# RMS norms moved in front of the feature-major projections, the last norm by token tile, and a first weight chunk that takes its tokens in halves

## The chip, the cores and the metric

The kernel runs on one core of a Trainium2 chip. The metric is the device time of one execution in microseconds (us). The kernel is one program with five engines that run side by side: TensorE (PE, with its weight loads as PEld), VectorE (DVE), ScalarE (ACT), GpSimd (POOL) and SyncE (SP), which issues most of the loads. They are kept in order by semaphores alone.

## The reference, cut to what matters

512 tokens of 1024 features pass through a first block (two attention layers with a mixture of experts, not touched here) and a second block of two layers. The second block, in float32, is

```python
for layer in range(DEPTH):                       # DEPTH = 2
    hn = rms_norm_2(h, norm_mix[layer])
    h = h + mixer(hn)                            # layer 0: retention and delta net; layer 1: rglru_mixer
    h = h + conv_ffn(rms_norm_2(h, norm_ffn[layer]), ffn_w_up[layer], ..., ffn_w_down[layer])
return rms_norm_2(h, norm_final)

def _rms(x):
    return x * lax.rsqrt(jnp.mean(x * x, axis=-1, keepdims=True) + EPS)
def rms_norm_2(x, gain):
    return _rms(x) * gain
```

`ffn_w_up` is 1024 x 5632, `ffn_w_down` 2816 x 1024 (22 rows of 128), `lru_w_in` 1024 x 2048.

## The kernel before, in words

The state X lies with tokens on the partitions: four tiles (T = 4) of 128 tokens x 1024 features. Every product of float32 matrices is made of three one-pass matmuls: each operand is split into a rounded part (hi) and a rest (lo), and `product` issues hi·hi, hi·lo and lo·hi. `raw(c)` and `hi(c)` are the two buffers of a weight chunk c: ACT rounds the raw chunk in two pieces (`round_chunk`), DVE puts the rest back over the raw one in two pieces (`rest_of_chunk`). There are two such pairs of buffers, so a chunk's load waits until the chunk before the last one is used up; SP issues it.

A feature-major projection (`linear_T`) keeps the weights still (128 x 128) and streams the 512 tokens, so it needs the normed X turned: XT (hi) and XH (lo) hold it as 8 blocks of 128 features by 512 tokens. Four places of the second block matter here, and I name them by letters:

- **A**: from `mix_out` (the last product of layer 0's mixer) to `ffn0_up`.
- **B**: from `ffn0_down` to `lru_in`, the first projection of layer 1's mixer.
- **C**: from `lru_out` to `ffn1_up`.
- **D**: from `ffn1_down` over the final norm to the store of `out`.

At A, B and C the order before is: DVE adds the last product to X (`residual`, `ffn_residual`), ACT squares all four tiles with a sum along the row (`squares`), POOL makes the reciprocal roots (`power`, L905 and L907), DVE multiplies each tile with its root into XH (`rms`, L2751), PE waits for all four tiles, bridged by some matmuls on constants (`keep_warm`, L1970), and turns them with 32 transposes (`turn`, L1795), one bank for each block of features over all tokens; ACT rounds each bank with the gain as its per-partition scale (`rounded_T`, L1111), DVE takes the rest (`rest_of_T`, L2678), and `linear_T` starts. The weights' first chunk is rounded on ACT before the squares and split on DVE before the scaling. A chunk of an up projection or of `lru_in` is four outputs of 24 matmuls with 512 columns.

`ffn` on PE then runs 11 chunks of up and, before the change, six chunks of down with 4, 4, 4, 4, 4 and 2 rows of 128; each chunk goes over four token tiles and two halves of the 1024 features, and `down_used` tells SP that a chunk is used up. The down product's left operand is `act` (rest) with `act_hi(f)`: rows 0 to 6 have their hi in a buffer `hi`, rows 7 to 14 in XT, rows 15 to 21 in XH.

At D the final norm scales by root and gain in one instruction (L3701) for each tile after all four are added, and one DMA stores all of `out`.

The PSUM banks are given out by a planner (`plan.take`, `plan.pick`), in turn.

## Time and profile before

| | |
|---|---|
| median of 3 runs | 3312.08 us (3310.1 to 3312.66) |
| span of the profiled execution | 3301.4 us |
| between the span and the median | 10.7 us, ahead of the first and after the last instruction |
| PE busy | 3133.6 us, 95% of the span |
| DVE, ACT, POOL busy | 2171.0, 1594.0, 415.7 us |
| mean granted TensorE clock | 0.982 |

The profiled execution has a span but no time of its own beside the three runs, so its own time is taken to be its span and the 10.7 us around it. "Start" in the rows is counted from the start of the span. L numbers are lines of the kernel before unless a row is said to be of the changed one, whose lines lie 10 to 70 further down.

### The profile page before, as it was taken

Reading aid. Unit: us, or ns where it says so; the run is one execution under the profiler, and the core shown is the slowest. Engines: PE = TensorE matmul, PEld = TensorE weight load, DVE = VectorE, ACT = ScalarE, POOL = GpSimd, SP = SyncE. Lnnn points to the kernel's source line nnn. Section 1 sums busy time; section 2 is a strip of 40 time slices with the busy share of each in tenths; the row PEclk is TensorE's granted clock in tenths of the full one; section 3 lists DMA queues with packets and bytes.
Section 4 is the critical chain, followed back from the end, with each engine's and each line's share of the span. In section 5 each row is a group of like instructions: output and inputs, shape, how many; then the busy total and the mean of one; then the engine's idle time right before and its main releaser. Section 6 shows DMA issues by size and latency. Waiting matters only on the chain.

```text
span 3301.4 us, 39275 instructions
## 1 busy us (share of the span) xinstructions
PE 3133.6 (95%) x14815; PEld 2391.1 (72%) x14815; DVE 2171.0 (66%) x2380; ACT 1594.0 (48%) x1889; POOL 415.7 (13%) x274
## 2 busy tenths in 40 slices
PE   8879999999998989899999999998899999999998
PEld 7556667777776867577777757877788887788886
DVE  2375578888885266688888876564477745757653
ACT  2465167777774344477777754342322212722211
POOL 0000122222212000222223220010000000000000
PEclk9999999999999999999999999999999999999999
DMA  7200389999993211699999973330123223223321
GB/s 263 106 1 14 149 309 361 351 358 360 359 355 134 77 46 65 249 363 348 356 361 351 360 279 73 76 65 1 60 94 98 82 101 102 77 83 102 102 102 64
DMA packets 174479, 599.20 MB, mean 181 GB/s; under 512 B 25571, under 2 KB 74899, under 8 KB 124947
## 3 DMA queue, kind: packets, MB, share of 16 engines
q1 hardware_dynamic: 140528, 541.75, 44.9%
q0 software_dynamic: 23472, 51.42, 4.4%
q10 hardware_dynamic: 10355, 4.33, 0.5%
q8 instruction: 83, 1.36, 0.2%
q14 instruction: 41, 0.34, 0.0%
HBM read 581.17 MB, written 48.23 MB: 191 GB/s over the span
## 4 chain that ended last, share of the span: by engine, by line
PE 78%; DVE 8%; DMA 6%; ACT 4%; issue 3%; POOL 1%; DVEq 0%; SPq 0%; ACTq 0%; POOLq 0%
PE bank L1820 20%; PE bank L1822 19%; PE bank L1821 19%; DMA ring<-w_gate 3%; PE bank L1832 3%; PE bank L2368 2%; PE bank L1884 2%; PE bank L1885 2%; PE bank L2118 1%; PE bank L1827 1%; PE bank L1828 1%; DVE st L2779 1%; PE bank L1945 1%; ACT ring_rounded L1276 1%; PE bank L2149 1%
## 5 line engine op out<-in xcount | busy, mean ns | idle before, releaser
L1821 PE MATMUL bank<-ring_rounded,big_rounded 128*96 128x512 f32 (+1 forms) x1680 | 660.1, 393 | 0.0
L3019 DVE TENSOR_TENSOR ring_rounded<-ring,big_rounded 128x2048 fp32r<-128x2048 f32 x252 | 568.1, 2287 | 42.2 <-ACT big_rounded L1276 41.3
L2666 DVE TENSOR_TENSOR ring_rounded<-ring,ring_rounded 128x2048 fp32r<-128x2048 f32 (+2 forms) x124 | 273.4, 2247 | 402.0 <-ACT ring_rounded L1096 401.9
L1276 ACT ACTIVATE big_rounded<-ring 128x2048 fp32r<-128x2048 f32 x252 | 478.6, 1918 | 74.2 <-DMA ring<-w_up 56.6
L1096 ACT ACTIVATE ring_rounded<-ring 128x2048 fp32r<-128x2048 f32 (+2 forms) x124 | 226.7, 1878 | 454.9 <-DMA ring<-ffn_w_down 163.6
L1820 PE MATMUL bank<-big_rounded 128*96 128x512 f32 x992 | 395.0, 398 | 1.0 <-DVE ring_rounded L3019 0.8
L3019 DVE TENSOR_TENSOR ring_rounded<-ring,ring_rounded 128x2048 fp32r<-128x2048 f32 x128 | 292.6, 2287 | 156.4 <-ACT ring_rounded L1276 148.1
L1822 PE MATMUL bank<-big_rounded,XH_rounded 128*96 128x512 f32 x992 | 392.1, 395 | 0.0
L1821 PEld LDWEIGHTS bank<-ring_rounded,big_rounded 128*96 128x96 f32 (+1 forms) x1680 | 277.5, 165 | 105.4
L1276 ACT ACTIVATE ring_rounded<-ring 128x2048 fp32r<-128x2048 f32 x128 | 245.1, 1916 | 208.3 <-DMA ring<-w_gate 208.0
L1822 PE MATMUL bank<-ring_rounded,XH_rounded 128*96 128x512 f32 (+1 forms) x776 | 307.2, 396 | 0.0
L1820 PE MATMUL bank<-ring_rounded,big_rounded 128*96 128x512 f32 (+1 forms) x688 | 276.2, 401 | 11.8 <-DVE XH_rounded L3028 4.9
L1820 PE MATMUL bank<-XT_rounded,ring_rounded 128*128 128x512 f32 x696 | 274.1, 394 | 2.4 <-DVE big L3108 2.4
L1821 PE MATMUL bank<-XH_rounded,ring_rounded 128*128 128x512 f32 x696 | 271.6, 390 | 0.0
L1822 PE MATMUL bank<-XT_rounded,ring_rounded 128*128 128x512 f32 x696 | 271.4, 390 | 0.0
L1820 PE MATMUL bank<-ring_rounded,XT_rounded 128*128 128x512 f32 (+1 forms) x584 | 228.7, 392 | 9.4 <-DVE XH_rounded L3450 3.9
L1822 PE MATMUL bank<-ring_rounded,big_rounded 128*128 128x512 f32 (+1 forms) x608 | 235.7, 388 | 0.0
L956 POOL DMA_INDIRECT expert_rows<-big,idx x64 | 118.2, 1847 | 865.8 <-ACT big L1298 809.3
L1821 PE MATMUL bank<-ring_rounded,XT_rounded 128*128 128x512 f32 (+1 forms) x584 | 227.0, 389 | 0.0
L1822 PEld LDWEIGHTS bank<-big_rounded,XH_rounded 128*96 128x96 f32 x992 | 159.8, 161 | 70.3
L1820 PEld LDWEIGHTS bank<-big_rounded 128*96 128x96 f32 x992 | 162.2, 164 | 66.9 <-DVE ring_rounded L3019 1.7
L905 POOL TENSOR_SCALAR st<-st 128x1 f32<-128x1 f32 (+3 forms) x43 | 16.4, 382 | 1523.0 <-ACT lnp L1355 918.6
(464 smaller groups left out, 5238.1 us busy)
## 6 DMA issues: line engine op xcount, KB each, us to landing
ring<-w_up SPq DMA_DIRECT2D x128, 1024.0 KB, 7.6
ring<-w_down SPq DMA_DIRECT2D x128, 1024.0 KB, 7.8
ring<-w_gate SPq DMA_DIRECT2D x128, 1024.0 KB, 7.0
ring<-ffn_w_up SPq DMA_DIRECT2D x44, 1024.0 KB, 6.9
ring<-ffn_w_down SPq DMA_DIRECT2D x10, 2048.0 KB, 7.8
ring<-ret_gdn_w_in SPq DMA_DIRECT2D x8, 2048.0 KB, 13.3
expert_rows<-lnp POOLq DMA_DIRECT2D x1, 12288.0 KB, 40.2
ring<-odd_w_qkv SPq DMA_DIRECT2D x6, 2048.0 KB, 8.0
```

Of the source, the lines that this page charges most:

```text
L956: pool.indirect_dma_start(expert_rows, bass.IndirectOffsetOnAxis(ap=used[0:CAP, e:e + 1], axis=0), M["YE"][0:CAP, e % 2, :], None, bounds_ ...
L1096: act.activation(one_pass(hi(c)[:, ks, :]), raw(c)[:, ks, :], ACT.Copy).then_inc(rounded[c.pair], 1)
L1276: act.activation(one_pass(expert_hi(j)), expert_raw(j), ACT.Copy).then_inc(signal("half_rounded").sem, 1)
L1820: pe.matmul(dst, x_hi, y_hi, start=first, stop=False)
L1821: pe.matmul(dst, x_hi, y_lo, start=False, stop=False)
L1822: return pe.matmul(dst, x_lo, y_hi, start=False, stop=last)
L1832: return pe.matmul(dst, one_pass(x_hi), one_pass(y_lo), start=False, stop=last)
L1884: pe.matmul(dst, w, one_pass(XT[:, kk, :].rearrange("p (t c) -> p t c", t=T)), start=(kk == 0), stop=False)
L1885: pe.matmul(dst, w, x_lo, start=False, stop=False)
L2368: ins = pe.matmul(ps(u)[:, tokens(h)], lhsT[:, h, :], rhs[:, h, :], start=start and (stop or h == 0), stop=stop and (start or h == GDN_HEA ...
L2666: dve.tensor_tensor(one_pass(w), w, parts(hi(c)[:, ks, :]), ALU.subtract).then_inc(split[c.pair], 1)
L3019: dve.tensor_tensor(one_pass(expert_raw(j)), expert_raw(j), parts(expert_hi(j)), ALU.subtract).then_inc(signal("half_split").sem, 1)
```

## The change

At A, B and C the norm is made tile by tile, with root and gain in one DVE instruction (`scaled_by_row`); the gain row comes by a POOL DMA into `lnp[:, 0, :]` (`load_gain`). Each tile is turned by 8 transposes into two banks of its own (`turn_tile`), and PE issues those of tiles 0, 1 and 2 behind tiles 1, 2 and 3 of the product that ends the stage before. The first chunk of the next projection (`first_T_by_halves`) runs its first three outputs over tokens 0 to 255 with 256-column matmuls, turns tile 3 behind the second of them, runs the same three over tokens 256 to 511, and the fourth over all 512. The constants' matmuls are gone. At D adding and scaling alternate by tile and each tile is stored by a DMA of its own. The down rows go in chunks of 3, 3, 4, 4, 4, 4; the last four rows keep their hi in `hi`, so XH is free for the next norm, and DVE waits for two used chunks before it writes them.

```diff
+DOWN_ROWS = [(0, 3), (3, 3)] + [(f, 4) for f in range(6, KF, 4)]
...
-        U["rmsf0_T"] = plan.take(KD)
+        U["rmsf0_T"] = [plan.pick(b) for b in (0, 1, 2, 3, 4, 6, 7, 5)]
...
+            if f >= KF - 4:
+                return F_["hi"][:, f - KF + 4, :]
...
@@ SP
-            sp.wait_ge(signal("out_ready").sem, signal("out_ready").next(sp, T))
-            sp.dma_start(out[0].rearrange("(t p) d -> p t d", p=P), XH[:, :, :]).then_inc(signal("out_stored").sem, 16)
+            for t in range(T):
+                sp.wait_ge(signal("out_ready").sem, signal("out_ready").next(sp))
+                sp.dma_start(out[0][t * P:(t + 1) * P, :], XH[:, t, :]).then_inc(signal("out_stored").sem, 16)
...
@@ POOL
+            def load_gain(gain):
+                pool.dma_start(next_gain_row, gain.partition_broadcast(P)).then_inc(signal("gain_loaded").sem, 16)
             if on(8):
+                load_gain(a["norm_ffn_2"][0])
                 rms()
             if on(9):
+                pool.wait_ge(signal("xh_ready").sem, 2 * T)
+                load_gain(a["norm_mix_2"][1])
                 rms()
...
@@ ACT
+            def squares_and_parts(name, uses, c):
+                square(uses, 0)
+                round_chunk(c)
+                square(uses, 1)
+                rounded_tile(name, 0)
+                square(uses, 2)
+                rounded_tile(name, 1)
+                square(uses, 3)
+                rounded_tile(name, 2)
+                rounded_tile(name, 3)
...
@@ PE
+            def first_T_by_halves(c, us, tiles, name):
+                for half in range(2):
+                    for t in (2 * half, 2 * half + 1):
+                        turned_tile(name, t)
+                    if half == 0:
+                        pe.wait_ge(split[c.pair], 2 * c.nth)
+                    at, ts = slice(2 * half * P, 2 * (half + 1) * P), slice(2 * half, 2 * half + 2)
+                    for q, (u, m) in enumerate(zip(us[0:3], tiles)):
...
+                        for kk in range(KD):
+                            ins = product(dst, hi(c)[:, kk, m * P:(m + 1) * P], raw(c)[:, kk, m * P:(m + 1) * P],
+                                          XT[:, kk, at].rearrange("p (t c) -> p t c", t=2), XH[:, ts, kk * P:(kk + 1) * P], kk == 0, kk == KD - 1)
+                        if half == 0 and q == 1:
+                            turn_tile(name, XH, T - 1, "xh_ready")
...
+                linear_T(c, us, tiles, None, 3)
...
                         if f == KF - 1:
                             ins.then_inc(full[u.bank], 1)
+                            if into and h and t:
+                                turn_tile(into, XH, t - 1, "xh_ready")
...
             if on(8):
-                keep_warm(U["rmsf0_T"][0], 3)
-                turn("rmsf0_T", XH, "xh_ready")
-                ffn(0)
+                ffn(0, "rms1_T")
             if on(9):
-                keep_warm(U["rms1_T"][0], 10)
-                turn("rms1_T", XH, "xh_ready")
+                first_T_by_halves(W["lru_in"][0], U["lru_in"][0], range(4), "rms1_T")
...
@@ DVE
+            def scaled_by_row(t, told):
+                dve.wait_ge(signal("rstd_ready").sem, signal("rstd_ready").next(dve))
...
+                dve.scalar_tensor_tensor(XH[:, t, :], X[:, t, :], rstd[:, t:t + 1], next_gain_row, ALU.mult, ALU.mult).then_inc(signal(told).sem, 1)
+            def normed_tiles(name, c, add):
+                add(0)
+                scaled_by_row(0, "xh_ready")
+                add(1)
+                rest_of_piece(c, 0)
+                scaled_by_row(1, "xh_ready")
+                rest_of_piece(c, 1)
+                add(2)
+                rest_of_tile(name, 0)
+                scaled_by_row(2, "xh_ready")
+                rest_of_tile(name, 1)
+                add(3)
+                rest_of_tile(name, 2)
+                scaled_by_row(3, "xh_ready")
+                rest_of_tile(name, 3)
...
+                    if n == KF - 4:
+                        dve.wait_ge(signal("down_used").sem, l * (len(DOWN_ROWS) - 1) + 2)
...
             if on(9):
-                rest_of_chunk(W["lru_in"][0])
-                rms()
-                rest_of_T("rms1_T", gain="norm_mix_2", gain_at=KD)
+                normed_tiles("rms1_T", W["lru_in"][0], lambda t: ffn_residual(0, t))
...
             if on(11):
...
+                    ffn_residual(1, t)
+                    scaled_by_row(t, "out_ready")
```

What the change moves is best seen at B; A and C are alike, with one add for each tile instead of two. On PE, before, between the last three matmuls of `ffn0_down` and the first of `lru_in`, stand the constants' matmuls and all transposes:

```order
L1820 MATMUL bank<-ring_rounded,XH_rounded 128x512
L1821 MATMUL bank<-ring_rounded,XH_rounded 128x512
L1822 MATMUL bank<-ring_rounded,big_rounded 128x512
L1970 MATMUL bank<-const 128x512 x10
L1795 MATMUL bank<-const,XH 128x128 x32
L1884 MATMUL bank<-XT_rounded,ring_rounded 128x512
L1885 MATMUL bank<-XH_rounded,ring_rounded 128x512
```

In the changed kernel PE has, at the same place (end of `ffn0_down`'s tile 3, L1840 to L1842 being `product`), the 8 transposes of tile 2 (L1978) and then matmuls of 256 columns:

```order
L1840 MATMUL bank<-ring_rounded,big_rounded 128x512
L1841 MATMUL bank<-ring_rounded,big_rounded 128x512
L1842 MATMUL bank<-ring_rounded,big_rounded 128x512
L1978 MATMUL bank<-const,XH 128x128 x8
L1840 MATMUL bank<-XT_rounded,ring_rounded 128x256
L1841 MATMUL bank<-XH_rounded,ring_rounded 128x256
L1842 MATMUL bank<-XT_rounded,ring_rounded 128x256
```

The transposes of tiles 0 and 1 have moved further up, behind tiles 1 and 2 of the last chunk, and those of tile 3 down, behind 48 of the 256-column matmuls. On DVE, before, B is one list by kind: adds (L2744), split of the chunk (L2666), scaling (L2751), rests of the turned blocks (L2678):

```order
L2744 TENSOR_TENSOR X<-X,bank 128x512 x8
L2666 TENSOR_TENSOR ring_rounded<-ring,ring_rounded 128x2048 x2
L2751 TENSOR_SCALAR XH<-X,st 128x1024 x4
L2678 SCALAR_TENSOR_TENSOR XH_rounded<-bank,chan,XT_rounded 128x4x128 x8
```

In the changed kernel the same place on DVE goes by tile (L2798 the adds, L2806 the scaling with root and gain, L2773 the pieces of the chunk, L2766 the rests of a turned tile):

```order
L2798 TENSOR_TENSOR X<-X,bank 128x512 x2
L2806 SCALAR_TENSOR_TENSOR XH<-X,st,lnp 128x1024
L2798 TENSOR_TENSOR X<-X,bank 128x512 x2
L2773 TENSOR_TENSOR ring_rounded<-ring,ring_rounded 128x2048
L2806 SCALAR_TENSOR_TENSOR XH<-X,st,lnp 128x1024
L2773 TENSOR_TENSOR ring_rounded<-ring,ring_rounded 128x2048
L2798 TENSOR_TENSOR X<-X,bank 128x512 x2
L2766 TENSOR_TENSOR XH_rounded<-bank,XT_rounded 128x512 x2
L2806 SCALAR_TENSOR_TENSOR XH<-X,st,lnp 128x1024
```

The scaling of a tile now stands between the adds of one tile and the next, and the rests of tile 0 stand ahead of the scaling of tile 2. On SP the last six loads of `ffn1_down` and the store before are

```order
L780 DMA ring<-ffn_w_down 128x4x1024 [waits down_used] x3
L780 DMA ring<-ffn_w_down 128x2x1024 [waits down_used]
L890 DMA out<-XH 128x4x1024 [waits out_ready]
```

and in the changed kernel

```order
L784 DMA ring<-ffn_w_down 128x4x1024 [waits down_used] x4
L895 DMA out<-XH 128x1024 [waits out_ready] x4
```

so that the last chunk has grown from two rows to four, and the store is four DMAs of a quarter's size.

## Rows read from the trace of the kernel before

**Rows 1.** The page, busy time of each engine, its share of the span, and instructions.

```profile
PE 3133.6 (95%) x14815; PEld 2391.1 (72%) x14815; DVE 2171.0 (66%) x2380; ACT 1594.0 (48%) x1889; POOL 415.7 (13%) x274
```

**Rows 2.** Timeline of PE at A: start us, us, engine, line, out<-in, count.

```profile
2389.82 2.74 PE L1970 MATMUL bank<-const 128*128 128x512 f32 x6
...
2399.59 0.48 PE L1884 MATMUL bank<-XT_rounded,ring_rounded 128*128 128x512 f32 x1
...
2420.10 0.39 PE L1820 MATMUL bank<-XT_rounded,ring_rounded 128*128 128x512 f32 x1
...
2421.46 0.39 PE L1884 MATMUL bank<-XT_rounded,ring_rounded 128*128 128x512 f32 x1
```

**Rows 3.** Timeline of PE at B.

```profile
2758.74 8.74 PE L1970 MATMUL bank<-const 128*128 128x512 f32 x20
...
2796.54 0.39 PE L1884 MATMUL bank<-XT_rounded,ring_rounded 128*128 128x512 f32 x1
```

**Rows 4.** Timeline of PE at C.

```profile
2920.40 2.73 PE L1970 MATMUL bank<-const 128*128 128x512 f32 x6
2925.03 3.71 PE L1795 MATMUL bank<-const,XH 128*128 128x128 f32 x32 [1.90 <-DVE XH L2751]
2928.50 0.48 PE L1884 MATMUL bank<-XT_rounded,ring_rounded 128*128 128x512 f32 x1
```

**Rows 5.** The chain at B, in order of time: start us, us, what.

```profile
2748.06 7.88 DMA ring<-lru_w_in
...
2760.87 1.21 POOL st L905
2762.16 2.48 POOL st L907
```

**Rows 6.** The chain at D, to the last instruction.

```profile
3287.92 0.70 DVE X L2744
3288.73 1.16 ACT lnp L1355 x2
3290.04 1.28 POOL st L905
3291.39 1.60 POOL st L907
3293.08 1.28 DVE XH L3701
```

**Rows 7.** DMA issues: count, KB each, median us from issue to landing.

```profile
ring<-ffn_w_down SPq DMA_DIRECT2D x10, 2048.0 KB, 7.8
out<-XH SPq DMA_DIRECT2D x1, 2048.0 KB, 6.6
ring<-even_w_ukv SPq DMA_DIRECT2D x1, 512.0 KB, 3.4
```

**Rows 8.** Timeline of PE in the one chunk of 416 columns, and a group by lines.

```profile
85.87 0.35 PE L1827 MATMUL bank<-ring_rounded,XT_rounded 128*128 128x416 f32 x1
...
87.18 0.35 PE L1828 MATMUL bank<-ring_rounded,big_rounded 128*128 128x416 f32 x1
...
L2072 PE MATMUL bank<-router,XT 128*128 128x36 f32 x128 | 14.8, 275 | 0.0
```

**Rows 9.** Groups and timelines: turned blocks rounded at A, POOL's pair at C, and the down stage.

```profile
L1111 ACT ACTIVATE XT_rounded<-bank,chan 128x512 fp32r<-128x512 f32 x8 | 5.2, 686 | 3.6 <-PE bank L1795 3.5
...
2915.48 0.19 POOL L905 TENSOR_SCALAR st<-st 128x1 f32<-128x1 f32 x1 [146.87 <-ACT lnp L1355]
2915.76 0.54 POOL L907 TENSOR_TENSOR st<-st,const 128x1 f32<-128x1 f32 x1
...
2668.82 3.72 ACT L1096 ACTIVATE ring_rounded<-ring 128x2048 fp32r<-128x2048 f32 x2 [18.04 <-DMA ring<-ffn_w_down]
2670.84 4.49 DVE L2666 TENSOR_TENSOR ring_rounded<-ring,ring_rounded 128x2048 fp32r<-128x2048 f32 x2 [11.46 <-ACT ring_rounded L1096]
```

**Rows 10.** Timeline of DVE near the end of layer 1's mixer.

```profile
2865.14 4.49 DVE L2666 TENSOR_TENSOR ring_rounded<-ring,ring_rounded 128x2048 fp32r<-128x2048 f32 x2 [0.34 <-ACT ring_rounded L1096]
```

More of the change, by code:

```diff
@@ L323, in plan_ffn @@
             plan_linear(f"ffn{l}_up", KF * FF_COLS, per_chunk=4, dmas=2)
-            n = (KF + 3) // 4
-            W[f"ffn{l}_down"] = [plan.chunk(min(4, KF - 4 * i), D, D) for i in range(n)]
+            n = len(DOWN_ROWS)
+            W[f"ffn{l}_down"] = [plan.chunk(nk, D, D) for _, nk in DOWN_ROWS]
             U[f"ffn{l}_down"] = plan.take(N_BANKS)
@@ L851, in load_ffn @@
                 down = a["ffn_w_down_2"][l].rearrange("(k p) n -> p k n", p=P)
-                for i, c in enumerate(W[f"ffn{l}_down"]):
-                    load(c, raw(c), down[:, 4 * i:4 * i + c.nk, :])
+                for (f, nk), c in zip(DOWN_ROWS, W[f"ffn{l}_down"]):
+                    load(c, raw(c), down[:, f:f + nk, :])
             sp.dma_start(X[:, :, :], a["x"][0].rearrange("(t p) d -> p t d", p=P)).then_inc(signal("x_loaded").sem, 16)
@@ L1344, in experts, with square, by_pair @@
                     act.wait_ge(late(l, "added"), EXPERTS * T)
-            def squares(uses, each=None):
-                for t in range(T):
-                    for u in uses[t] if uses else ():
-                        act.wait_ge(drained[u.bank], u.n + 1)
-                    if each:
-                        act.wait_ge(signal(each).sem, signal(each).next(act))
-                    unread = y_sq if uses else XH[:, t, :]
-                    act.activation(unread, X[:, t, :], ACT.Square, accum_out=ssq[:, t:t + 1]).then_inc(signal("x_ssq").sem, 1)
-                    act.wait_ge(signal("x_ssq").sem, signal("x_ssq").next(act))
+            def square(uses, t):
+                for u in uses[t]:
+                    act.wait_ge(drained[u.bank], u.n + 1)
+                act.activation(y_sq, X[:, t, :], ACT.Square, accum_out=ssq[:, t:t + 1]).then_inc(signal("x_ssq").sem, 1)
+                act.wait_ge(signal("x_ssq").sem, signal("x_ssq").next(act))
+            def squares_and_parts(name, uses, c):
[8 more added lines that the diff above has]
+                rounded_tile(name, 3)
             def by_tile(name):
                 return list(zip(*U[name]))
+            def by_pair(name):
+                return [U[name][2 * t:2 * t + 2] for t in range(T)]
             def ffn(l):
@@ L1684, in _ @@
             if on(8):
[L1685 to L1687 removed]
+                squares_and_parts("rmsf0_T", by_tile("mix_out"), W["ffn0_up"][0])
                 ffn(0)
             if on(9):
[L1690 to L1691 removed]
+                squares_and_parts("rms1_T", by_pair("ffn0_down"), W["lru_in"][0])
                 for i, v in enumerate((a["lru_w_a_2"], a["lru_w_x_2"])):
                     load(L_["w"][:, i, :, :], v[0].rearrange("n i j -> i n j"), "gates_loaded")
[L1694 removed]
                 act.wait_ge(signal("lam_arg").sem, signal("lam_arg").next(act))
@@ L1774, in _ @@
             if on(10):
-                round_chunk(W["ffn1_up"][0])
-                squares(by_tile("lru_out"))
-                rounded_T("rmsf1_T", gain="norm_ffn_2", gain_at=KD)
+                squares_and_parts("rmsf1_T", by_tile("lru_out"), W["ffn1_up"][0])
                 ffn(1)
             if on(11):
-                squares([U["ffn1_down"][2 * t:2 * t + 2] for t in range(T)])
+                for t in range(T):
+                    square(by_pair("ffn1_down"), t)
         @block.tensor
@@ L2630, in _ @@
                         ins.then_inc(full[u.bank], 1)
+                        if i == 1 and t:
+                            turn_tile("rmsf1_T", XH, t - 1, "xh_ready")
             if on(10):
-                keep_warm(U["rmsf1_T"][0], 3)
-                turn("rmsf1_T", XH, "xh_ready")
-                ffn(1)
+                ffn(1, None)
         @block.vector
```

108 lines of the change are left out of this document (56 added, 52 removed).

## The prediction

> **What bounds the kernel now.** I read the busy times first: PE is busy for 95% of the span [rows 1], so only PE's work, or a time in which PE does nothing useful, can move the end. Then I read PE's timeline at the four places. At A the product before ends at 2389.82, where the constants' matmuls begin, and the first chunk of the next projection runs from 2399.59 to 2421.46 [rows 2]: 31.64 us in all, of which 21.87 are the chunk's 96 matmuls (six of them from 2420.10 to 2421.46, so 0.2267 each, and 5.44 for 24). At B the same stretch is 2758.74 to 2796.54, 37.80 us [rows 3]. At C it is 2920.40 to 2928.50 and the chunk [rows 4], 8.10 + 21.88 = 29.98 us. In these stretches PE stands, multiplies constants or turns all of XH at once. B is longer because of the chain [rows 5]: the load of `lru_in`'s first chunk starts when the second last down chunk is used up (2748.06) and takes 7.9 us, while the last chunk has only 2 rows, 8 x 2 x 3 matmuls or 10.9 us; ACT rounds that chunk ahead of the squares, and POOL's first pair then takes 1.21 + 2.48 us beside DVE's splitting. At D the chain [rows 6] runs one tile through add, square, POOL, scaling; it ends 3294.36, the store's 6.6 us [rows 7] and 0.4 us of closing end the span at 3301.4.
>
> **PE's work in the new stretch.** It is the same for A, B and C, counted from the end of the product without any transposes: 32 transposes at 3.71 / 32 = 0.116 us [rows 4] are 3.7 (C's price, since they now stand in a dense stream). The fourth output is 24 x 0.2267 = 5.4. The other three outputs are 2 x 3 x 24 = 144 matmuls of 256 columns instead of 72 of 512. No such split matmul is in the trace. Eight of 416 columns start from 85.87 to 87.18, 0.187 apart [rows 8], those of 512 columns 0.2267 apart [rows 2], so a column costs 0.00041 and a matmul 0.015 besides: 256 columns make 0.121. From below, a matmul of just 36 columns with its own 128-column weight load costs 14.8 / 128 = 0.116 [rows 8], as the 128-column transposes do: that is the weight load's own pace. I take 0.121, between 0.116 and 0.187. 144 x 0.121 = 17.4. The sum is 3.7 + 5.4 + 17.4 = 26.5 us of PE work.
>
> **The gains if PE never waits** are therefore: A 31.6 - 26.5 = 5.1, B 37.8 - 26.5 = 11.3, C 30.0 - 26.5 = 3.5, together 19.9 us.
>
> **The waits that may take their place.** I walked through B with the rows' durations, from the start of the last down chunk as 0: it has now 4 rows, so a token tile ends every 5.44 us and `lru_in`'s load (7.9) lands at 7.9, inside it. Durations: from a tile's end to the add 0.26, add 0.70, square 1.16, POOL's pair about 0.8 when DVE leaves it alone [rows 9], scaling with the row 1.28 [rows 6], a piece of the chunk 1.86 on ACT and 2.25 on DVE, a turned bank's rounding 0.69 [rows 9], its rest like an add 0.70, a tile's 8 transposes 0.93.
> Tile 0 is scaled at about 10.4 and PE wants it at 10.9. Tile 1: its add ends 11.9, its square 13.1, but POOL's operation lies beside the first piece of the chunk on DVE (to 14.2), so root and scaling are done at 15.1 and 16.4; PE wants it at 17.3. Tile 2: the second piece ends 18.7, the adds 20.1, the rest of tile 0 21.6, root 22.4, scaled 23.8; PE wants it at 23.6 and waits 0.3. The rest of tile 1 ends 25.2 where PE's first half could start at 24.9: 0.4. Tile 3 is added at 26.6, squared 27.9, and scaled after the rest of tile 2, 31.3, where PE has come through two outputs at 31.15: 0.3. Its rest is done at 34.6, ahead of the second half (35.3). I allow 1.1 us at B. At A and C only one add stands between (the other half was added earlier), tile 2 is scaled 0.6 us before PE wants it, and I allow 0.1 each. Together 1.3, so A to C give 18.6 us. This is a chain with under 1 us of slack at five places; cover gone, each microsecond on DVE or POOL is paid at all three.
>
> At one point a rule of the Trainium skill speaks against the change. The page "SBUF — State Buffer", section "Who interferes with whom", says that a VectorE instruction with two SBUF inputs and a GpSimd instruction that reads SBUF lock each other out for a whole instruction. The trace agrees, with the 1.21 + 2.48 us of POOL's pair beside DVE's splitting against 0.19 + 0.54 alone [rows 5, 9]. By that rule each root computed beside a piece of the chunk is late by up to one DVE instruction, which is what I put in for tile 1.
>
> **D.** The last tile's chain was 0.26 from PE's end to the add (3287.66 to 3287.92), then to 3294.36: 6.7 us, with 1.28 + 1.60 in POOL while DVE scaled the three tiles before. Now those are scaled earlier, DVE is idle, and the pair takes 0.8: 0.26 + 0.70 + 0.1 + 1.16 + 0.15 + 0.8 + 0.1 + 1.28 = 4.6, 2.1 less. A tile's own chain of 4.6 fits in the 5.44 between tiles (with 2 rows it was 2.72). The last store has 512 KB instead of 2048; the nearest row of this size takes 3.4, the whole one 6.6 [rows 7]. I take 3.4: 3.2 less, and zero if size did nothing. D gives 5.3 us.
>
> **Edits at nothing.** Down rows 3, 3, 4, ... : PE's total is the same. The third chunk's load now starts 3 rows, 16.3 us, after down begins and must be split 32.6 after: 16.3 + 7.8 [rows 7] + 6.5 (2668.82, where ACT had waited for the load, to 2675.3, the end of DVE's two instructions) [rows 9] = 30.6, 2.0 us of cover; a load of 9.8 us would use it up, in two ffns. DVE's wait for two used chunks (32.6) is far ahead of the 98 at which PE reads those rows. The gain rows' DMAs on POOL's queue are issued whole stages ahead (after the norm before, after the last scan), behind nothing but POOL's roots. The constants' matmuls were no work. `lru_w_a`'s two loads are now issued on ACT behind the norm, 20 us before PE's first gate. Layer 1's mixer: PE's chunk end pulls the loads, and DVE waited 0.34 for ACT's rounding of the one for `lru_out` [rows 10], so that stage hangs from PE and moves up with it; DVE's first convolutions come at most 3 us later against PE, and its next wait for ACT takes most of this.
>
> **Sum.** 5.1 + 11.3 + 3.5 - 1.3 + 5.3 = 23.9 us. The profiled span of 3301.4 becomes 3277.5; with the 10.7 us around it, which make it the median of 3312.1, **3288.2 us**.
>
> **Rivals.**
> 1. *The halves cost far more than half* (ends on the other side). If a 256-column matmul takes the 0.187 us of the nearest row, 432 of them cost 432 x 0.066 = 28.5 us more: 3316.7, slower. It decides from 0.121 + 23.9 / 432 = 0.176 us each. Against it: 128 and 36 columns both go at 0.116 with a weight load each, and nothing in the rows says why 256 columns should exceed both that and their own columns' time. 4%.
> The Trainium skill, page "TensorE: Matmul & The Clock Gate", section "Back-to-back issue gap", gives pairs of weight load and matmul as about 81 ns for 128 columns and 131 ns for 512. A straight line between them puts 256 columns at 0.745 of the 512-column cost, which would be an estimated 0.169 us here and a time of about 3309 us. The trace has 0.227 us for 512 columns, not 0.131, and its 0.116 for 36 columns is about half of that, so I count this rule within the 4%.
> 2. *The tile chain is late at each turn.* If POOL's pair takes the slow 3.7 instead of 0.8 at every tile, DVE's list is late by 2.9 per tile, at most some 8 per site less about 1 of slack; a DVE instruction blocks POOL only to its end, so I price it at 3.5 a site instead of the 1.3 for all: +9 us, 3297. For it: the order on DVE is strict, and the slack is under 1 us. 15%.
> 3. *Layer 1's mixer swallows B.* If its DVE and ACT chain keeps its own time, B's 11.3 - 1.1 = 10.2 is lost and the time is 3298.4. For it: only 0.34 us between DVE's last scan and its next work. Against it: both hang from loads that PE's progress releases. 8%.
> 4. *The third down chunk is late, or the store doesn't shrink*: 2 to 4 us, 3292. 10%, held inside the likeliest one's range.
>
> **Numbers.** The forecast 3288.2 with rival 4 has 73%, rivals 2 and 3 23%, rival 1 4%. The likeliest one's own range is 3284.7 (0.116 us for the halves saves 2.2, no waits 1.3) to 3293. For 8 in 10 I reach over rivals 2 and 3 above and leave out rival 1 and both tails: 3283 to 3299. A change of 0.2% (6.6 us) is about what a measurement of this kernel tells from none. Faster by more: 0.95; within it, most of all by the page's 3309 or several rivals at once: 0.02; slower: 0.03.
>
> **What would show it.** Matmuls of 256 columns start 0.12 apart; if 0.17 or more, rival 1. PE has gaps of under 0.5 us ahead of the transposes of tiles 2 and 3 at B and none at A; if they are 2 us or more and end on the scaling, rival 2. The stretches at A, B and C, from the end of the product (transposes inside it added) to the end of the chunk, are 26.6, 27.6 and 26.6. From PE's last matmul to the last scaling 4.6 us, and to the end 8.4. The stretch from `lru_in`'s second chunk to C is as long as before (123.9 us from 2796.54 to 2920.40, with 1.9 of transposes added), else rival 3. Any PE idle in the down stage is rival 4. The prediction is wrong if PE's clock falls in the new stretches, or if the chain at B keeps POOL's 3.7 us.

## The result, and the profile after

| | before | changed |
|---|---|---|
| median, first set of runs | 3311.09 us (3308.45 to 3312.66, 4 runs) | 3288.17 us (3283.25 to 3291.79, 4 runs), ratio 0.9943, 95% [0.9926, 0.9960] |
| median, a later set (experiments 10 and 11) | 3302.28 us (3293.4 to 3309.72, 11 runs) | 3284.12 us (3279.08 to 3290.52, 6 runs), ratio 0.9950, 95% [0.9934, 0.9966] |
| profiled execution | span 3301.4 us | span 3289.7 us, its own time 3291.79 us |
| A, B, C (end of the product to end of the chunk) | 31.64, 37.80, 29.98 us | 26.31, 26.97, 26.31 us |
| PE's last matmul to the span's end | 13.74 us | 11.47 us |

The change made the kernel faster, by 22.9 us in the first set, where 23.9 were predicted, and by 18.2 in the later one. That the first median, 3288.17 us, meets the forecast of 3288.2 so closely is luck. The agreement hides this: the stretches A to C gave 19.8 us instead of 18.6, of which 3.3 are time that PE lost to a lower clock in the profiled execution of the kernel before, and D gave 2.3 instead of 5.3.

Those 3.3 us stand in the turning of XH before, at A and B: behind PE's wait for the last scaling the granted clock fell to 0.50, PE's lower level of 1.2 GHz, and the 32 transposes took 5.38 us instead of the 3.71 at C ([rows 4]), where the clock stayed at 1.00 behind a wait of the same 1.90 us. PE's timeline of the kernel before at A and B:

```profile
2394.45 5.38 PE L1795 MATMUL bank<-const,XH 128*128 128x128 f32 x32 [1.90 <-DVE XH L2751]
...
2769.53 5.38 PE L1795 MATMUL bank<-const,XH 128*128 128x128 f32 x32 [2.04 <-DVE XH L2751]
```

and its granted clock inside the first (window, length, busy us and instructions of PE, PEld, DVE, ACT, POOL, then PEclk, DMA share, GB/s):

```profile
2396.00:2398.00 2.00, 2.00 (x11) 2.00 (x10) 1.99 (x3) 1.77 (x3) 0.00 (x0) 0.50 0.80 251
```

PE's timeline of the changed kernel at A (start us, us, engine, line, out<-in, count) answers to [rows 2]:

```profile
2401.85 1.04 PE L1978 MATMUL bank<-const,XH 128*128 128x128 f32 x8
2402.64 0.36 PE L1840 MATMUL bank<-XT_rounded,ring_rounded 128*128 128x256 f32 x1
...
2403.08 0.28 PE L1840 MATMUL bank<-XT_rounded,ring_rounded 128*128 128x256 f32 x1
2403.20 0.28 PE L1841 MATMUL bank<-XH_rounded,ring_rounded 128*128 128x256 f32 x1
2403.32 0.28 PE L1842 MATMUL bank<-XT_rounded,ring_rounded 128*128 128x256 f32 x1
...
2408.47 1.03 PE L1978 MATMUL bank<-const,XH 128*128 128x128 f32 x8
...
2426.32 0.39 PE L1904 MATMUL bank<-XT_rounded,ring_rounded 128*128 128x512 f32 x1
```

The product ends at 2401.85 with two tiles' transposes inside it (0.92 each, so 1.84 are added to the stretch); the third tile's transposes follow it directly, the matmuls of 256 columns start 0.120 us apart, the last tile's transposes stand in their middle with no bracket behind them (no wait), and the second chunk begins at 2426.32: 2426.32 - 2401.85 + 1.84 = 26.31 us.

The same view at B, answering to [rows 3], where one small wait is left, the 0.4 that I had allowed for there:

```profile
2765.42 1.03 PE L1978 MATMUL bank<-const,XH 128*128 128x128 f32 x8
2766.87 0.35 PE L1840 MATMUL bank<-XT_rounded,ring_rounded 128*128 128x256 f32 x1 [0.41 <-DVE XH_rounded L2766]
...
2790.55 0.39 PE L1904 MATMUL bank<-XT_rounded,ring_rounded 128*128 128x512 f32 x1
```

C has no wait (answers to [rows 4]):

```profile
2916.47 1.03 PE L1978 MATMUL bank<-const,XH 128*128 128x128 f32 x8
...
2940.94 0.39 PE L1904 MATMUL bank<-XT_rounded,ring_rounded 128*128 128x512 f32 x1
```

PE's waits in the changed kernel from A to the end of the span (waiting line, what it waited for, us, times, longest):

```profile
PE bank L1840 <- DVE big_rounded L3727: 0.9, 2, 0.6
PE bank L1840 <- DVE XH_rounded L2766: 0.4, 1, 0.4
```

The 0.9 us lie in layer 1's mixer, where 0.6 were before; the waits of [rows 4] are gone.

At D the chain answers to [rows 6], and the closing instructions of two queues (in this view: line, queue, operation, count: ns min/median/max, first and last start) show what the prediction did not have:

```profile
3278.49 0.70 DVE X L2798
3279.29 1.16 ACT lnp L1364 x2
3280.87 0.55 POOL st L912
3281.52 1.28 DVE XH L2806
```

```profile
L190 POOLq DRAIN  x1: 7829/7829/7829, 3281.6 to 3281.6; - x1
...
L190 SPq DRAIN  x1: 7/7/7, 3285.6 to 3285.6; - x1
L190 SPq EVENT_SEMAPHORE  x1: 17/17/17, 3289.6 to 3289.6; - x1
```

POOL's pair now takes 0.2 + 0.55 us. The last scaling ends at 3282.8, 4.6 us after PE's last matmul, whose end is taken as 0.26 us ahead of the add, as in the prediction (3278.23). The store lands at 3285.4. But SP then stands until 3289.6: POOL's queue, done with its last root at 3281.4, is in a DRAIN (an instruction that stands at the close of every queue) of 7.8 us, and the program ends when all queues have met. In the kernel before that DRAIN lasted from 3293.2 to 3300.8 and the 2048 KB store landed at about 3301.0, so the two ended together and the chain of [rows 6] showed only the store.

### The profile page after: what moved, and what is told of

It reads as the page before. It is cut to its first block, busy times and chain, and to the rows that moved or that the text cites. A ratio compares the mean times of both kernels' runs of the same rounds, so it can differ in the third digit from the quotient of the medians.

```text
span 3289.7 us, 39679 instructions
## 1 busy us (share of the span) xinstructions
PE 3124.1 (95%) x14999; PEld 2397.1 (73%) x14999; DVE 2177.3 (66%) x2380; ACT 1592.2 (48%) x1889; POOL 404.8 (12%) x277
## 4 chain that ended last, share of the span: by engine, by line
PE 78%; DVE 8%; DMA 6%; ACT 4%; issue 3%; POOL 1%; DVEq 0%; SPq 0%; POOLq 0%; ACTq 0%
PE bank L1840 20%; PE bank L1842 20%; PE bank L1841 20%; DMA ring<-w_gate 3%; PE bank L1852 3%; PE bank L2414 2%; PE bank L1904 1%; PE bank L1905 1%; PE bank L2138 1%; PE bank L1847 1%; PE bank L1848 1%; ACT ring_rounded L1290 1%; PE bank L1965 1%; PE bank L2169 1%; DVE st L2851 1%
## 5 line engine op out<-in xcount | busy, mean ns | idle before, releaser
L1841 PE MATMUL bank<-ring_rounded,big_rounded 128*96 128x512 f32 (+1 forms) x1744 | 685.3, 393 | 0.0
L2713 DVE TENSOR_TENSOR ring_rounded<-ring,ring_rounded 128x2048 fp32r<-128x2048 f32 (+2 forms) x118 | 260.4, 2246 | 375.0 <-ACT ring_rounded L1110 374.9
L1840 PE MATMUL bank<-big_rounded 128*96 128x512 f32 x992 | 395.0, 398 | 1.2 <-DVE ring_rounded L3091 1.0
L1842 PE MATMUL bank<-big_rounded,XH_rounded 128*96 128x512 f32 x992 | 392.0, 395 | 0.0
L1841 PEld LDWEIGHTS bank<-ring_rounded,big_rounded 128*96 128x96 f32 (+1 forms) x1744 | 289.3, 166 | 107.6
L1840 PE MATMUL bank<-ring_rounded,big_rounded 128*96 128x512 f32 (+1 forms) x752 | 301.4, 401 | 12.9 <-issue 5.6
L1842 PE MATMUL bank<-ring_rounded,XH_rounded 128*96 128x512 f32 (+1 forms) x776 | 307.8, 397 | 0.0
L1840 PE MATMUL bank<-XT_rounded,ring_rounded 128*128 128x512 f32 (+1 forms) x792 | 297.1, 375 | 2.8 <-DVE big L3180 2.4
L1841 PE MATMUL bank<-XH_rounded,ring_rounded 128*128 128x512 f32 (+1 forms) x792 | 294.1, 371 | 0.0
L1842 PE MATMUL bank<-XT_rounded,ring_rounded 128*128 128x512 f32 (+1 forms) x792 | 293.9, 371 | 0.0
L1840 PE MATMUL bank<-ring_rounded,XT_rounded 128*128 128x512 f32 (+1 forms) x584 | 229.4, 393 | 9.7 <-DVE XH_rounded L3524 3.9
L1842 PE MATMUL bank<-ring_rounded,big_rounded 128*128 128x512 f32 (+1 forms) x608 | 235.7, 388 | 0.0
L961 POOL DMA_INDIRECT expert_rows<-big,idx x64 | 106.5, 1665 | 876.4 <-ACT big L1312 824.4
L1840 PEld LDWEIGHTS bank<-big_rounded 128*96 128x96 f32 x992 | 162.1, 163 | 67.4 <-DVE ring_rounded L3091 2.4
L1842 PEld LDWEIGHTS bank<-big_rounded,XH_rounded 128*96 128x96 f32 x992 | 159.7, 161 | 70.3
L953 POOL DMA_INDIRECT big<-expert_rows,idx x64 | 184.3, 2879 | 57.0 <-PE bank L2138 31.6
```

Of the source, the lines that this page charges most:

```text
L953: pool.indirect_dma_start(M["XE"][0:CAP, e % 2, :], None, expert_rows, bass.IndirectOffsetOnAxis(ap=used[0:CAP, e:e + 1], axis=0), bounds_ ...
L961: pool.indirect_dma_start(expert_rows, bass.IndirectOffsetOnAxis(ap=used[0:CAP, e:e + 1], axis=0), M["YE"][0:CAP, e % 2, :], None, bounds_ ...
L1840: pe.matmul(dst, x_hi, y_hi, start=first, stop=False)
L1841: pe.matmul(dst, x_hi, y_lo, start=False, stop=False)
L1842: return pe.matmul(dst, x_lo, y_hi, start=False, stop=last)
L2713: dve.tensor_tensor(one_pass(w), w, parts(hi(c)[:, ks, :]), ALU.subtract).then_inc(split[c.pair], 1)
```

## Experiments

"A, B, C" are the stretches of the table. "Tail" is the time from PE's last matmul (0.26 us ahead of the last add) to the span's end. Totals of single executions move by more than most effects here (last section), so I judge by stretches. For the record, the single executions gave 3282.17 us (experiment 1), 3277.54 (3), 3312.49 (4), 3302.03 (5), 3305.72 (6), 3284.90 (7), and 3320.38 and 3309.14 (8 and 9).

**1. One store at the end.**

```
-            for t in range(T):
-                sp.wait_ge(signal("out_ready").sem, signal("out_ready").next(sp))
-                sp.dma_start(out[0][t * P:(t + 1) * P, :], XH[:, t, :]).then_inc(signal("out_stored").sem, 16)
-            sp.wait_ge(signal("out_stored").sem, signal("out_stored").next(sp, 16 * T))
+            sp.wait_ge(signal("out_ready").sem, signal("out_ready").next(sp, T))
+            sp.dma_start(out[0].rearrange("(t p) d -> p t d", p=P), XH[:, :, :]).then_inc(signal("out_stored").sem, 16)
+            sp.wait_ge(signal("out_stored").sem, signal("out_stored").next(sp, 16))
```

> The changed kernel with the output stored in one transfer of 2048 KB after the last tile, as before the change, instead of four of 512 KB. Read from PE's last matmul to the end of the span, which is 11.5 us in the changed kernel. Theory (POOL's closing DRAIN of 7.8 us, which begins after POOL's last root, ends the span, not the store): the large store lands some 6.6 us after the last scaling, which is 4.6 us after PE's last matmul, so at about 11.3 us, hidden by the drain: 11.5 us again, within 0.4. Rival (the last store sets the end, and the small ones were worth their 3 to 4 us): 15 us.

Measured: tail 11.56 us (last add at 3268.70, span 3280.0). The store takes 6.6 us, and it costs nothing. The closing rows of this kernel:

```profile
L190 POOLq DRAIN  x1: 7829/7829/7829, 3271.8 to 3271.8; - x1
...
L190 SPq DRAIN  x1: 7/7/7, 3279.8 to 3279.8; - x1
```

POOL's DRAIN ends at 3279.6, and SP is ready at 3279.8, 0.2 us later: the large store ends with the DRAIN, and splitting it bought 0.1 us. That it is the DRAIN which hides the size, and not that size never counts, the next two show.

**2. The final roots off POOL.** DVE makes the mean square and its reciprocal, ACT the square root.

```
                 load_gain(a["norm_final_2"])
-                rms()
...
                     square(by_pair("ffn1_down"), t)
+                    act.wait_ge(signal("ms_ready").sem, signal("ms_ready").next(act))
+                    act.activation(rstd[:, t:t + 1], rstd[:, t:t + 1], ACT.Sqrt).then_inc(signal("rstd_ready").sem, 1)
...
+            def mean_square(t):
+                r = rstd[:, t:t + 1]
+                dve.wait_ge(signal("x_ssq").sem, signal("x_ssq").next(dve) + 4 * T)
+                dve.tensor_scalar(r, ssq[:, t:t + 1], 1.0 / D, RMS_EPS, ALU.mult, ALU.add).then_inc(dve_done.sem, 1)
+                dve.wait_ge(dve_done.sem, dve_done.next(dve))
+                dve.reciprocal(r, r).then_inc(signal("ms_ready").sem, 1)
...
                     ffn_residual(1, t)
+                    mean_square(t)
                     scaled_by_row(t, "out_ready")
```

> The changed kernel with the final norm's four roots taken from POOL: DVE makes the mean square and its reciprocal, ACT the square root, and DVE scales as before. POOL has nothing left to do after its last gain load at site C. Theory (POOL's DRAIN ends the span): the drain lies far ahead, and from PE's last matmul to the end of the span it takes the chain of 4.6 us, the store of 512 KB of 2.6 us and 0.1 to 0.3 around it: 7.4 us, 4.1 less than 11.5; the total falls by about 4 us (ratio 0.9988). Rival (the drain belongs to the end of the program, and starts when the last engines are done whatever POOL did): 11.5 us or more, no change of the total. In both, a table load of ACT for the square root can show, at the first tile, beside PE's work.

Measured: tail 7.8 us (last add 3270.20, span 3277.7), median 3285.84 us (6 runs, 3274.82 to 3290.02), ratio to before 0.9942 [0.9923, 0.9961]. The DRAIN now starts some 360 us ahead of the end, and SP's comes last:

```profile
L190 POOLq DRAIN  x1: 8458/8458/8458, 2914.1 to 2914.1; - x1
...
L190 SPq DRAIN  x1: 7/7/7, 3277.5 to 3277.5; - x1
```

The tail is 3.7 us shorter where 4.1 were expected: the chain to the last scaling took 4.25 us instead of 4.6, but the last of the four stores took 3.1 us here instead of 2.6, which I can't explain. The rival falls: the DRAIN follows POOL's own last work and does not wait for the program's end.

**3. The same with one store.** The edit of experiment 1 on the kernel of experiment 2.

> The kernel with the roots taken from POOL (as in the run before this one), and the output in one store of 2048 KB. Theory (the drain hid the store's size, and without the drain the size counts): from PE's last matmul to the end of the span 4.6 + 6.6 + 0.2 = 11.4 us, 4.0 more than with four stores. Rival (the drain comes at the end whatever POOL does): the same 11.5 us or more as with four stores and roots off POOL.

Measured: tail 12.1 us (last add 3263.96, span 3275.8), with a store of 7.4 us where 6.6 were expected. Without the DRAIN the store's size is worth 12.1 - 7.8 = 4.3 us; with it, 11.56 - 11.47 = 0.1. The four kernels together show the hidden term. Why POOL's DRAIN lasts so long, no run shows.

**4. No halves.**

```
-                for half in range(2):
-                    for t in (2 * half, 2 * half + 1):
-                        turned_tile(name, t)
...
-                linear_T(c, us, tiles, None, 3)
+                turn_tile(name, XH, T - 1, "xh_ready")
+                for t in range(T):
+                    turned_tile(name, t)
+                linear_T(c, us, tiles)
```

> The changed kernel without the halves: at A, B and C PE transposes the last tile as soon as it is scaled, waits for all four, and takes the first chunk in products of 512 columns. Read by the stretches that took 26.3 (A), 27.0 (B) and 26.3 us (C). Theory (the halves cover the last tile's chain): the last tile is scaled 4.6 us after the product's end and rounded 2.6 us after its transposes begin, so PE idles about 6.3 us, less 1.0 that the 144 products of 256 columns cost over 72 of 512: A 31.6, B 32, C 31.6, 16 us more in all. Rival (the gain comes from scaling in front and from the rows, and the halves add little): each stretch within 1.5 us of now.

Measured: A 34.36, B 37.12, C 34.21 us, so 26.1 more than with halves. A single execution gave 3312.49 us, beside 3307.38 for the kernel before. PE's timeline at A, and its granted clock there:

```profile
2396.06 1.03 PE L1978 MATMUL bank<-const,XH 128*128 128x128 f32 x8
2401.54 1.62 PE L1978 MATMUL bank<-const,XH 128*128 128x128 f32 x8 [4.44 <-DVE XH L2792]
2404.88 0.76 PE L1904 MATMUL bank<-XT_rounded,ring_rounded 128*128 128x512 f32 x1 [1.72 <-DVE XH_rounded L2752]
```

```profile
2400.00:2403.00 3.00, 1.46 (x8) 1.22 (x8) 1.48 (x2) 0.60 (x1) 0.60 (x1) 0.82 1.07 357
2403.00:2406.00 3.00, 1.28 (x4) 0.96 (x4) 1.38 (x2) 1.57 (x2) 0.00 (x0) 0.50 0.76 252
2406.00:2409.00 3.00, 3.00 (x9) 2.35 (x8) 2.04 (x1) 2.98 (x3) 0.00 (x0) 0.54 0.00 0
2409.00:2412.00 3.00, 3.00 (x14) 2.45 (x14) 2.46 (x2) 1.03 (x1) 0.00 (x0) 1.00 0.00 0
```

The waits are 4.44 + 1.72 = 6.2 us, as worked out (6.3). What I had not counted comes on top: behind the idle time the granted clock is 0.50, PE at its lower level of 1.2 GHz. The eight transposes take 1.62 us instead of 1.03 and the chunk, to its successor at 2428.58, 23.70 us instead of 21.87, about 2.4 us in all. B idles for 5.9 + 1.7 us. At A and C this kernel is 2.7 and 4.2 us slower than the one before, and at B 3.2 us slower than experiment 6, which has the rows alone: the scaling in front and the norm by tiles are a loss without the halves that cover the last tile.

**5. Down rows 4,4,4,4,4,2.**

```
-DOWN_ROWS = [(0, 3), (3, 3)] + [(f, 4) for f in range(6, KF, 4)]
+DOWN_ROWS = [(f, min(4, KF - f)) for f in range(0, KF, 4)]
```

> The changed kernel with the down rows in chunks of 4,4,4,4,4,2 as before, so that the last chunk lasts 10.9 us instead of 21.8. Theory: at B lru_in's load is issued 11 us later against the product's end, ACT rounds it in front of the square of tile 1, and that tile and the two behind it come late on DVE: the first product of 256 columns starts about 10 us after the product's end instead of 0.4, so B goes from 27.0 to 36 or 37 us. At D a tile's add and scaling take DVE 5.3 us in all with the waits in between, and a tile now comes every 2.7: from PE's last matmul to the span's end 19 us instead of 11.5. A and C stay. Rival (only the wait for the load itself counts, the tiles' chain keeps up): B 27 to 31 us, D within 1 us.

Measured: A and C 26.31 us. From A's second chunk to B's it is 374.15 us instead of 364.23 (2426.32 to 2790.55), so B has 9.9 us more: 36.9. Tail 18.5 us. PE's waits at B:

```profile
PE bank L1978 <- DVE XH L2806: 7.8, 3, 4.1
PE bank L1840 <- DVE XH_rounded L2766: 0.5, 1, 0.5
```

Both parts of the theory stand. The waits are 8.3 us where 0.4 were; much of the rest is the clock again, which was granted at 0.50 from 2761 to 2764, behind the wait of 4.1 us (the eight transposes there take 1.97 us). The tile-wise norm lives on a tile time of 5.4 us; at 2.7 a tile's own chain is longer than the tile (at D one scaling follows the other by 5.07 us), and it costs 9.9 us at B and 7.0 at D.

**6. The rows alone, in the kernel before.** DOWN_ROWS of the change and nothing else.

> The kernel before with nothing changed but the down rows, 3,3,4,4,4,4. Theory (at B the late load and the squares behind its rounding were what B had over C): B's 37.8 us falls by about 7.8 to C's 30; A (31.6), C (30.0) and the stretch after PE's last matmul (13.7) stay within 0.3. Rival (the rows matter only together with the norm by tiles): B stays at 36 us or more.

Measured: A 29.99, B 33.92 (constants' matmuls from 2765.27, second chunk at 2799.19), C 29.98 us, tail 13.7. So the rows alone give 3.9 at B, half of the 7.8 expected, and A, which nothing in this edit touches, is 1.7 us below the 31.6 expected. PE's transposes at A and B in this kernel:

```profile
2402.64 3.71 PE L1796 MATMUL bank<-const,XH 128*128 128x128 f32 x32 [1.90 <-DVE XH L2752]
...
2773.85 3.71 PE L1796 MATMUL bank<-const,XH 128*128 128x128 f32 x32
```

A differs by the clock alone: the same wait of 1.90 us, but a granted clock of 1.00 behind it and 3.71 us for the transposes instead of 5.38. At B, the transposes start 8.6 us after the product's end instead of 10.8, which is 2.2 us, and the other 1.7 are the clock: with no wait ahead of them the transposes run at 1.00. The load is no longer late (ACT rounds the chunk from 2751.62, 13.7 us before the product's end). What still holds B 3.9 us above C is DVE's order. DVE and POOL in this kernel:

```profile
2766.26 4.49 DVE L2667 TENSOR_TENSOR ring_rounded<-ring,ring_rounded 128x2048 fp32r<-128x2048 f32 x2
2770.67 3.12 DVE L2752 TENSOR_SCALAR XH<-X,st 128x1024 f32<-128x1024 f32 x4
...
2767.65 0.95 POOL L906 TENSOR_SCALAR st<-st 128x1 f32<-128x1 f32 x1 [4.62 <-ACT lnp L1356]
2768.68 2.77 POOL L908 TENSOR_TENSOR st<-st,const 128x1 f32<-128x1 f32 x1
```

The splitting still stands behind the last add, and all four scalings behind the splitting; they end at 2773.8, when the constants' matmuls end too. The last root beside the splitting takes 3.7 us instead of 0.73, as in [rows 5], but it is done at 2771.45, before its tile's turn on DVE (2773.0), so here it costs nothing. The theory was half right at B, missed A by the clock, and the rival was wrong.

**7. The scaling twice.** Tiles 1 to 3 at A, B and C are scaled twice with the same operands.

```
+                if t and told == "xh_ready":
+                    dve.scalar_tensor_tensor(XH[:, t, :], X[:, t, :], rstd[:, t:t + 1], next_gain_row, ALU.mult, ALU.mult).then_inc(dve_done.sem, 1)
+                    dve.wait_ge(dve_done.sem, dve_done.next(dve))
```

> The changed kernel with the scaling of tiles 1, 2 and 3 done twice on DVE at A, B and C, so 1.28 us more for each tile. Theory (DVE's order of work has nothing to spare there, followed through row by row: the second scaling of tile 1 pushes the add and the scaling of tile 2, and what PE waits for first is tile 2's scaling and tile 1's rounding): PE waits about 2.3 us in front of the first half and 0.8 at the last tile's transposes, 3.1 us at each site: A 29.4, B 30.2, C 29.4. Rival (the tile's chain has the 1.2 us to spare that lie between the last tile's scaling and its transposes at A): under 0.6 us at each site.

Measured from tile 0's transposes to the second chunk, 37.17, 37.82 and 37.18 us in the changed kernel: A 40.06, B 41.96, C 40.05, so 2.9, 4.1 and 2.9 us more. PE at B waits for what was expected:

```profile
PE bank L1978 <- DVE XH L2809: 2.1, 2, 1.9
PE bank L1840 <- DVE XH_rounded L2766: 0.5, 1, 0.5
```

One instruction of 1.28 us a tile costs over twice its length at a site. This does not test POOL's pair, the cause that rival 2 of the prediction named, but it shows how little slack the chain has for it. B's 4.1 us have two parts. The first half starts 2.7 us later. Its 48 matmuls of 256 columns then take 7.31 us, to the last tile's transposes, instead of 5.83: from 2756.5 to 2759.7 they start 0.213 us apart, and the granted clock is at its lower level:

```profile
2757.00:2758.00 1.00, 1.00 (x7) 1.00 (x7) 0.00 (x0) 1.00 (x2) 0.00 (x0) 0.50 1.05 410
```

At A and C, behind waits of 1.2 + 0.5 us, it did not fall. The expectations for A and C (29.4) were met within 0.2 us; B's 31.1 (27.0 + 4.1) is 0.9 above its 30.2, which the clock's 1.5 more than covers.

**8, 9. Constants' matmuls in the wait.** On the kernel of experiment 4, to see whether its extra time is the clock. In the second version the numbers are 6 and 4:

```
+                keep_warm(U[name][2 * (T - 1)], 12 if name == "rms1_T" else 9)
                 turn_tile(name, XH, T - 1, "xh_ready")
```

> The kernel without the halves once more, with products of constants (9 at A and C, 12 at B, as the kernel before had them at this place) in front of the last tile's transposes. Without them the stretches took 34.4, 37.1 and 34.2 us, where PE's waits of 6.2, 7.6 and 6.2 us and the products alone give 31.6 to 32. Theory (the rest is the clock: after the idle time the transposes and the first products ran at 1.2 GHz, a granted clock of 0.50 in the 6 us behind the wait): with the products of constants the granted clock stays above 0.9 and A, B and C take about 31.8, 33.3 and 31.8 us. Rival (the rest comes from DVE and ACT, whose rounding delays PE's start whatever its clock is): the stretches stay above 33.5 at A and C.

> The kernel without the halves with 4 products of constants at A and C and 6 at B (9 and 12 took 7.9 and 9.3 us, about 0.9 each, and so lengthened the wait they should fill). 4 take 3.6 of the 4.4 us in which PE stood at A and C, 6 take 5.5 of 5.9 at B. Theory (what the stretches without halves have over work and waits is the clock): the last tile's transposes run at the full clock, which saves 0.7 us at A and C and 1.0 at B; the first products still follow an idle 1.7 us, after which the clock fell at A and C in the run before and did not at B, so A and C come to 32 to 33.7 us instead of 34.3, B to 34.5 to 36. Rival (the products of constants change nothing, or only delay): A and C stay at 34.2 or more, and B at 37.

With 9 and 12 of them: A 36.92, B 38.82, C 36.92 us, longer and not shorter. The first expectation failed by my count: one costs about 0.9 us (two instructions in the trace), so they overfilled the wait. With 4 and 6: A 33.84, B 35.32, C 33.69, which is 0.5, 1.8 and 0.5 less than without; A is 0.1 us above the range expected, B and C are inside theirs. A and C stay 2.2 and 3.7 us slower than in the kernel before, so the missing constants' matmuls are only a small part (0.5 us) of what experiment 4 lost to it. The transposes now run at full clock, but at A the chunk still loses 1.6 us; granted clock of the run with 4:

```profile
2402.00:2404.00 2.00, 0.91 (x8) 0.67 (x7) 0.79 (x2) 1.08 (x2) 0.60 (x1) 1.00 1.16 356
2404.00:2406.00 2.00, 1.14 (x4) 1.01 (x5) 0.50 (x1) 1.24 (x1) 0.00 (x0) 0.90 0.72 246
2406.00:2408.00 2.00, 2.00 (x6) 1.55 (x5) 1.29 (x1) 2.00 (x2) 0.00 (x0) 0.50 0.00 0
```

PE starts the chunk at full clock after an idle 1.95 us and drops to the lower level about a microsecond into it. In the run with 12 at B the same idle 1.95 us brought no drop: 2787.53 to 2809.40, 21.87 us. So the clock does carry part of what experiment 4 lost, and constants' matmuls give back a part of it; when the drop comes after so short a pause stays open.

**10, 11. The changed kernel and the roots off POOL on one chip.** No edits beyond those above.

> The changed kernel itself, timed on the same chip in the same rounds as the kernel with the roots off POOL. The stretches A, B and C as in its first profile (26.3, 27.0, 26.3, within 0.3), 11.5 us from PE's last matmul to the span's end, and a total of 3288 within 5 us, since the part in front of A has moved by up to 16 us from one execution to another.

> The kernel with the final roots off POOL, beside the changed kernel on the same chip. Theory: 3.7 us shorter after PE's last matmul in its profile (7.8 against 11.5), and the totals apart by about that much, which the spread of 5 us or more between executions can hide. Rival (the removed wait is paid again elsewhere): no difference in the stretch behind PE's last matmul.

Measured: the changed kernel A 26.31, B 26.95, C 26.33, tail 11.5, median 3284.12. Roots off POOL: tail 7.8 (last add 3264.47, span 3272.0), median 3278.83 us (3269.98 to 3285.03, 6 runs), ratio to before 0.9932 [0.9913, 0.9951]. In this set its median is the lower one by 5.3 us, but the intervals of the ratios overlap; in the earlier sets the two ratios to the kernel before were alike (0.9942 and 0.9943). That it is faster than the changed kernel rests on the 3.7 us in the profiles.

## Why the prediction was right, and where it was not

- **The halves' price** (0.121 us for 256 columns): 0.120. Rival 1 and its 0.187 are out, and so is the estimate of 0.169 us worked out from the Trainium skill, page "TensorE: Matmul & The Clock Gate", section "Back-to-back issue gap": here 256 columns with a weight load each stand at 0.53 of the 512-column time, not at 0.745.
- **PE's work** (26.5 us): A and C took 26.31 with no wait, so the gains are 5.3 and 3.7 instead of 5.1 and 3.5.
- **The stretches before** (31.6 and 37.8 us at A and B): the prediction took them from one execution and the transposes' price from C (3.71). So it had 1.7 us of lower clock at each of A and B in its gains without naming them. The changed kernel has no wait there behind which the clock could fall, so they are gained against this execution; experiment 6, where A took 29.99 with the same instructions, shows that not every execution has them to lose.
- **The waits** (1.3 us): 0.4, at B only. The walk through B held within a microsecond: counted from the load's issue (2742.03), the four scalings end at 9.7, 16.0, 23.2 and 30.3 us, forecast 10.4, 16.4, 23.8 and 31.3. Tile 0 was 0.7 us early already, before POOL and DVE had anything beside each other, so the difference is not POOL's; the durations put in were a little long. POOL's first operation of tile 1 took 0.97 us instead of 0.19: it began at 2755.09 beside a piece of the chunk on DVE and ended at 2756.06, 0.05 us after that piece, and the second took its 0.54. That is what the prediction said, "a DVE instruction blocks POOL only to its end". The Trainium skill, page "SBUF — State Buffer", section "Who interferes with whom", says that a VectorE instruction with two SBUF inputs and a GpSimd instruction that reads SBUF lock each other out; the trace agrees here and in experiment 6, where the second operation took 2.77 us beside the second piece.
- **B's 11.3 us**: 10.8. Its makeup was told rightly as far as the load goes, but experiment 6 shows that the rows are worth only 3.9 alone (1.7 of them the clock), and experiment 5 that the new order is worth next to nothing without them at B (37.8 to 36.9). Each needs the other.
- **D** (5.3 us, of which 3.2 from the smaller store): 2.3. This is the step that failed, although the total came out: "The last store has 512 KB instead of 2048 ... 3.2 less". The store did shrink, to 2.6 us, below the 3.4 of its nearest row. What I took for the only end of the span, the store and "0.4 us of closing", ran beside POOL's DRAIN of 7.6 us, which ended 0.2 us before it. POOL's DRAIN moves with POOL's last root, which came 5.3 us behind PE's last matmul before (3293.0) and 3.2 us now (3281.4): 2.1 us, and about 0.2 from what lay behind it. Experiments 1 to 3 show it both ways. Rival 4 had "the store doesn't shrink", with the right size and the wrong mechanism.
- **The 10.7 us around the span** were not around it. In every profiled run of these experiments 1.7 to 2.2 us lie there. The other 8 to 9 must then belong to the execution that was profiled before, which would have run that much below the median; its A starts 8.2 us earlier than in experiment 6 (2389.82 against 2398.00), with the same instructions in front. It did no harm, since the sum took a difference from the median.
- **The constants' matmuls "were no work"**: true where the halves leave PE no pause. PE's granted clock is 1.00 in all three new stretches. Experiments 4, 8 and 9 show the clock falling where a pause is left.
- **Rivals 3 and 4**: from B's second chunk to C it is 124.08 us (123.9 forecast; the waits in the mixer are 0.9 us instead of 0.6), and from A's second chunk to the end of B's product, transposes taken out, it is 337.26 us, 337.28 before. The mixer swallowed nothing and the third down chunk was not late.

The sum by stretches is 19.8 + 2.3 = 22.1 us; the medians are 22.9 and 18.2 us apart in the two sets. Without the 3.3 us of clock it would be 18.8; how often the kernel before loses them is not shown.

## What to carry to other kernels

Before costing a smaller last store, look at how each queue ends, not only at the chain that ended last: an engine's closing DRAIN can end within 0.2 us of the store and keep the whole gain. Give that engine's last work to another one, and the store's size counts again. When a norm is taken apart by tiles, compare the chain of a tile (here 4.6 to 5.1 us) with the time between tiles where the product ends, and see what PE has to do while the last tile is on its way: the tile time and the halves were worth more than the norm's new place. And before a stretch is priced from one trace, read its granted clock: A and B held 1.7 us each that another execution of the same instructions did not have.

## What the runs showed of the hardware

- POOL's closing DRAIN lasted 7.58 us after POOL's last root in the kernel before, 7.83 in the changed one, and 8.46 where POOL's last work was the issue of the gain's load. On ACT, DVE and SP it was 0.01 to 0.21 us; on PE's queue 4.27 us, over some 0.2 us after PE's last matmul and so hidden.
- After PE had stood for 1.90 to 2.04 us the granted clock fell to 0.50 in some places and not in others. It fell at A and B of the kernel before, at A, B and C with 4 and 6 constants' matmuls, at A and C with 9, and at B of experiment 7; it stayed at 1.00 at C of the kernel before, at A and C of experiment 6, at B with 12, and at B of experiment 5 behind its last long wait. A fall cost 1.5 to 1.7 us each time. What decides is open.
- A store of 512 KB landed in 2.6 us and one of 2048 KB in 6.6; with the roots off POOL the last ones took 3.1 and 7.4.
- The same instructions ahead of A, touched by none of these edits, ended up to 16.5 us apart from one execution to another: tile 0's transposes at A start at 2389.15 in the changed kernel's first profile, 2376.71 in its second, and 2372.61 in experiment 7. The last two ran on different chips, and the first one's is not on record, so the chip may have a part in it. This is why experiment 7, which adds 9.9 us by its stretches, had a lower single total (3284.9 us) than the changed kernel's first median.
